# Key projections on an unnormalized residual: a norm deferred past two units of a three-layer kernel

## The chip, the cores and the metric

One core of a Trainium2 chip runs the whole program in one launch. The metric is the device time of that launch in microseconds, as the median of the runs shown. Matrix products run on TensorE (PE), element-wise work on VectorE (DVE), ScalarE (ACT) and GpSimd (POOL), and SyncE's queue (SP) loads the weights. The engines run their own instruction streams in order and meet at semaphores.

## The reference, cut to what matters

Three attention layers follow each other, and a feed-forward layer after the first. The change lies between the second attention layer (differential attention, "A") and the third (windowed grouped-query attention, "B"). The residual is `x` (512 tokens, 1024 features) beside a context `ctx` of 256 tokens.

```
x   = x   + gate_x * (ox @ w_o[0])          # second output projection
ctx = ctx + gate_c * (oc @ w_o[0])
hx  = rms_norm(x,   norm_g[1]) * (1 + scale_x) + shift_x
hc  = rms_norm(ctx, norm_g[1]) * (1 + scale_c) + shift_c
q, k, v, g = split(hx @ w_in)               # 1024, 256, 256, 1024 columns
k   = rope(k); q = rope(q)                  # context keys are not rotated
```

`rms_norm` divides every token by the root of its mean square over the 1024 features. That factor is one number per token, so a product with the unnormalized tile `x * norm_g * (1 + scale_x)` can be multiplied by it afterwards, and the product of `shift_x` with the weights is added as one number per output column.

## The kernel before

**Layout and units.** Features lie on the 128 partitions and tokens in the free dimension, so the residual is `hc`, 8 tiles of 128 features by 768 tokens (512 of `x`, 256 of context). Every projection is cut into units of 128 output columns. A unit multiplies 8 weight tiles by 8 activation tiles; every float32 operand is split into a high and a low part, and `products` (L350) issues three matmuls of 512 (or 256) columns per tile: high by high, high by low, low by high.

**Weights.** SP loads a unit's raw weights into one of four slots. ACT makes the high part (`split_high`, L322, its instruction at L340), POOL the low part (`low`, L986). There are two slots for split weights, so `split_high` of unit u+2 waits until PE has finished unit u. PE waits for the low part.

**Around the change.** The output projection of layer A is done for seven of eight tiles while the heads still run. The last tile follows in `last_out` (L1289): 16 outputs n of three matmuls, 8 for `x` and 8 for the context, each added to `hc` by DVE (L2346). ACT squares the finished tiles (L1752), POOL sums five of them (L1025, L1028), PE sums over features with matmuls of one column (`column_sums`, L422, at L425), ACT takes the root (L431), DVE the reciprocal (L435), and PE spreads it over the partitions into PSUM bank 7 (`spread`, L437, at L440). All engines meet at the end of this phase. Then `modulated` (L2171) makes the normalized tiles one by one: DVE multiplies (`x_tile`, L2039), ACT adds the shift and rounds to the high part (`shift_tile`, L1555), DVE makes the low part (`low_tile`, L2045). PE takes up units 0 and 1 of layer B in `staggered` (L1129), unit 1 six tiles behind unit 0.

**Layer B's 20 units** are 8 for q, 2 for k, 2 for v and 8 for the gate. DVE rotates q and k in PSUM (L2381 to L2387), ACT rounds the high part (`take_b`, L1767, at L1780 or L1783) and DVE subtracts for the low one (L2392, L2396). The units of k and v also have 256 context columns. The context tiles are normalized in pairs during units 3 to 6. `take_b(u)` waits for unit u, splits the weights of unit u+2, and only then waits for the rotation of unit u, so ACT's queue ties the split of later weights to DVE's rotations. The order in every engine's queue is written out by hand.

## Time and profile before

| | us |
|---|---|
| median of 3 runs | 1624.75 |
| lowest and highest run | 1624.64, 1624.96 |
| the profiled execution's own time | 1624.65 |
| its span, first to last instruction | 1622.8 |
| mean granted TensorE clock | 0.986 |

The page of the profile gives each engine's busy time over the span and its share in 40 equal slices, the granted clock of TensorE in tenths, and the chain of work that ended last. The trace answers in more detail: the chain in order of time, single instructions of an engine with their start and duration, and busy time in chosen stretches. Times count from the start of the span.

### The profile page before, as it was taken

How to read it: one execution, taken by the hardware profiler on the slowest of the kernel's cores; microseconds unless marked ns; L12 is line 12 of the kernel's file. 1: busy time of each engine (PE TensorE's matmuls, PEld its weight loads, DVE VectorE, ACT ScalarE, POOL GpSimd, SP SyncE). 2: the span in 40 equal slices, each digit the busy share in tenths (PEclk: the TensorE clock that was granted, in tenths of full speed). 3: DMA queues.
4: the chain of work that ended last, by engine and by line, in shares of the span. 5: the costliest groups of instructions: out<-in, count | busy, mean ns of one | idle time of the engine just before them, and what ended most of it. 6: DMA issues, size and time to landing. Idle time of an engine off the chain costs nothing.

```text
span 1622.8 us, 23738 instructions
## 1 busy us (share of the span) xinstructions
PE 1553.3 (96%) x8400; PEld 1219.6 (75%) x8400; DVE 999.5 (62%) x2286; ACT 757.4 (47%) x1426; POOL 505.3 (31%) x231
## 2 busy tenths in 40 slices
PE   7998999999899999999989999999999989999997
PEld 5886666678688888888877877778777768866666
DVE  6235546355679867645787666675667267147854
ACT  6225676634342323233434544455445443248753
POOL 3651232245244444444221111221114343330012
PEclk9999999999999999999999999999999989999999
DMA  6861111263356665643210111111111122220001
GB/s 201 176 161 34 59 59 63 89 258 130 104 189 196 187 201 188 198 137 94 76 53 27 40 40 39 39 41 36 44 34 53 53 67 86 71 66 15 1 19 60
DMA packets 48402, 149.35 MB, mean 92 GB/s; under 512 B 5782, under 2 KB 9110, under 8 KB 48184
## 3 DMA queue, kind: packets, MB, share of 16 engines
q1 hardware_dynamic: 37080, 112.45, 22.8%
q10 hardware_dynamic: 11232, 35.72, 6.7%
q8 instruction: 54, 0.88, 0.2%
q14 instruction: 36, 0.29, 0.1%
HBM read 141.53 MB, written 6.62 MB: 91 GB/s over the span
## 4 chain that ended last, share of the span: by engine, by line
PE 79%; DVE 8%; ACT 6%; issue 5%; POOL 1%; DMA 1%; ACTq 0%; POOLq 0%; DVEq 0%; SPq 0%
PE ps L357 40%; PE ps L361 19%; PE ps L583 4%; PE ps L594 3%; PE ps L564 3%; PE ps L1336 3%; PE ps L1377 3%; PE ps L1348 1%; POOL w_l L986 1%; ACT sb L649 1%; PE ps L1091 1%; ACT w_h L340 1%; PE ps L425 1%; DVE tg L1972 1%; DVE b_sb L688 1%
## 5 line engine op out<-in xcount | busy, mean ns | idle before, releaser
L986 POOL TENSOR_TENSOR w_l<-raw,w_h 128x1024 fp32r<-128x1024 f32 (+1 forms) x190 | 457.7, 2410 | 894.8 <-ACT w_h L340 874.6
L340 ACT ACTIVATE w_h<-raw 128x1024 fp32r<-128x1024 f32 x190 | 200.5, 1057 | 351.8 <-PE ps L357 293.6
L357 PE MATMUL ps<-x1h,w_h 128*128 128x512 f32 x584 | 237.1, 406 | 16.1 <-POOL w_l L986 10.4
L357 PE MATMUL ps<-x2h,w_h 128*128 128x512 f32 (+2 forms) x784 | 234.0, 361 | 12.3 <-DVE x2l L2045 4.4
L357 PE MATMUL ps<-x1h,w_l 128*128 128x512 f32 x584 | 229.9, 394 | 0.0
L361 PE MATMUL ps<-x1l,w_h 128*128 128x512 f32 x584 | 229.2, 393 | 0.0
L361 PE MATMUL ps<-x2l,w_h 128*128 128x512 f32 (+2 forms) x784 | 221.5, 346 | 0.0
L357 PE MATMUL ps<-x2h,w_l 128*128 128x512 f32 (+2 forms) x784 | 221.2, 345 | 0.0
L357 PEld LDWEIGHTS ps<-x2h,w_h 128*128 128x128 f32 x784 | 126.6, 189 | 41.2 <-issue 12.8
L357 PEld LDWEIGHTS ps<-x2h,w_l 128*128 128x128 f32 x784 | 126.9, 189 | 19.6
L357 PEld LDWEIGHTS ps<-x1h,w_h 128*128 128x128 f32 x584 | 111.0, 190 | 40.4 <-POOL w_l L986 10.8
L361 PEld LDWEIGHTS ps<-x2l,w_h 128*128 128x128 f32 x784 | 126.6, 189 | 18.8
L357 PEld LDWEIGHTS ps<-x1h,w_l 128*128 128x128 f32 x584 | 110.7, 190 | 24.2
L361 PEld LDWEIGHTS ps<-x1l,w_h 128*128 128x128 f32 x584 | 111.2, 190 | 20.4
L2111 DVE CUSTOM_DVE_ANT_0 terms<-mraw,ps 128x1024 f32<-128x1024 f32 x96 | 116.8, 1216 | 2.5
L2280 DVE CUSTOM_DVE_ANT_0 a_p<-ps,small 128x768 f32<-128x768 f32 (+1 forms) x96 | 71.2, 775 | 59.3 <-issue 59.3
L357 PE MATMUL ps<-m_h,w_h 128*128 128x512 f32 x256 | 99.7, 389 | 0.0
L357 PE MATMUL ps<-m_h,w_l 128*128 128x512 f32 x256 | 99.6, 389 | 0.0
L361 PE MATMUL ps<-m_l,w_h 128*128 128x512 f32 x256 | 99.6, 389 | 0.0
L1686 ACT ACTIVATE a_p<-a_p,small 128x768 f32<-128x768 f32 (+1 forms) x96 | 75.2, 785 | 30.9 <-DVE small L2280 30.9
L993 POOL TENSOR_TENSOR g_stage<-g_stage,rstd 128x512 f32<-128x512 f32 x16 | 20.6, 1285 | 147.7 <-ACT g_stage L880 147.7
L688 DVE CUSTOM_DVE_ANT_0 b_sb<-ps,bm 128x512 f32<-128x512 f32 (+1 forms) x64 | 45.9, 753 | 25.9 <-PE ps L564 25.9
(344 smaller groups left out, 2713.5 us busy)
## 6 DMA issues: line engine op xcount, KB each, us to landing
raw<-in_w_mlp SPq DMA_DIRECT2D x64, 512.0 KB, 3.7
mraw<-in_w_mod ACTq DMA_DIRECT2D x51, 512.0 KB, 3.7
raw<-in_w_a SPq DMA_DIRECT2D x32, 512.0 KB, 3.6
raw<-in_w_att SPq DMA_DIRECT2D x25, 512.0 KB, 11.4
raw<-in_w_b SPq DMA_DIRECT2D x20, 512.0 KB, 3.6
raw<-in_w_g SPq DMA_DIRECT2D x16, 512.0 KB, 3.6
raw<-in_w_ao SPq DMA_DIRECT2D x9, 512.0 KB, 3.6
gates<-g_stage ACTq DMA_DIRECT2D x16, 256.0 KB, 2.1
```

The costliest lines, as they stand in the source:

```text
L340: nc.scalar.activation(split(u)[0], raw[:, u % RAW], ACT.Copy).then_inc(w_hi, 1)
L357: mm = nc.tensor.matmul(o, w[:, k], xh(k), start=(first and k == k0 and wi == 0), stop=(last and k == k1 - 1 and wi == 1))
L361: mm = nc.tensor.matmul(o, w[:, k], xl(k), start=False, stop=False)
L564: mm = nc.tensor.matmul(A.sbank(m + h)[:, o:o + rhs.shape[-1]], st[qx](r + h), rhs, start=(x == 0), stop=(x == last), skip_group_check=True)
L583: mm = nc.tensor.transpose(ps[0:w, 4 + x % A.tb, y * P:(y + 1) * P], A.sb[n % A.sbn][:, r, o:o + w], ident[:])
L594: mm = nc.tensor.matmul(ps[h * HD:(h + 1) * HD, 6 + g % 2, cols], st["v"](h)[b], A.pt[0:w, x % 4, h * 2 * P:(h + 1) * 2 * P], start=(st["f ...
L688: nc.vector.tensor_tensor_reduce(out=A.sb[n % A.sbn][:, r, 0:st["keys"]], in0=A.sbank(m)[:, st["off"]:st["off"] + st["keys"]], in1=st["bia ...
L986: nc.gpsimd.tensor_tensor(l[:, ks], raw[:, u % RAW, ks], h[:, ks].bitcast(F32), ALU.subtract).then_inc(w_lo, 1)
L1336: mm = nc.tensor.matmul(pair(1 + 2 * m)[:, o:o + n], aq[ms, qt * P:(qt + 1) * P], ak[ms, key:key + n], start=(x == 0), stop=(x == 2))
L1686: nc.scalar.activation(buf, buf, ACT.Exp, bias=negm[:, cc:cc + 1], scale=-1.0, accum_out=sums[:, cc:cc + 1]).then_inc(ha["e"], 1)
L2111: nc.vector.tensor_tensor_reduce(out=terms[:], in0=mraw[:, c % MRAW].rearrange("p k m -> p (k m)"), in1=cps[:, w, :], scale=0.5, scalar=0. ...
L2280: nc.vector.tensor_tensor_reduce(out=a_p[qt % 3][m][:, 0:n], in0=pair(1 + 2 * m)[:, 0:n], in1=zero.to_broadcast([P, n]), scale=1.0, scalar ...
```

## The change

The two key units move to the front of layer B and read unnormalized tiles of `x` (`xqh`, `xql`) and of the context (new halves in `x2h`, `x2l`). Two columns with the shifts ride along with the context (256 + 2 columns). Their results stay in PSUM banks 0 to 3 and are multiplied by the token factor there, given the shift, and rotated (`rotate_k`). The factor is spread a second time, into bank 4 (bank 6 for the context), and copied to `rstd` by ACT. The first tiles of the first key unit are put among the last outputs of `last_out`. The barriers "heads" and "ao" go. The q units read normalized tiles as before, from the third unit on.

The diff, cut to what sets order and work:

```diff
-        PHASES = ["prep", "wout", "heads", "ao"]
+        PHASES = ["prep", "wout"]
@@ gpsimd
-            add_squares(nm4, SQ_ADDED, 0, S)
             low(U_B)
+            add_squares(nm4, 1, SQ_ADDED, 0, S, sq4[0:2])
             low(U_B + 1)
-            add_squares(nm4c, N_OUT, S, SC)
-            lows(U_B + 2, U_END)
+            add_squares(nm4c, 1, 4, S, SC, sq4c)
+            low(U_B + 2)
+            add_squares(nm4c, 4, N_OUT, S, SC, sq4c)
+            lows(U_B + 3, U_END)
@@ tensor
+            def unscaled_x(j, k0, k1):
+                return products(U_B + j, [(ps[:, 2 * j], lambda k: xqh[:, k, :], lambda k: xql[:, k, :])], k0, k1,
+                                first=(k0 == 0), last=(k1 == KT), ready=lambda k: nm4p.wait(pe, "lo", k + 1))
+            def unscaled_ctx(j):
+                return products(U_B + j, [(ps[:, 2 * j + 1, 0:C + 2], lambda k: x2h[:, k, S:SC + 2], lambda k: x2l[:, k, S:SC + 2])],
+                                ready=lambda k: nm4cp.wait(pe, "lo", k + 1)).then_inc(unit, 1)
+            last_out(0, 12)
+            split_ready(pe, U_B)
+            unscaled_x(0, 0, 1)
+            last_out(12, 14)
+            unscaled_x(0, 1, 2)
+            last_out(14, 16)
+            unscaled_x(0, 2, 6)
+            nm4.wait(pe, "add", SQ_ADDED - 1)
+            column_sums(sqsum, 6, S, True, False)
...
+            mm.then_inc(nm4.mm, 1)
+            unscaled_x(0, 6, KT)
+            split_ready(pe, U_B + 1)
+            unscaled_x(1, 0, 3)
+            nm4.wait(pe, "rc", 1)
+            spread(7, 0, 4).then_inc(nm4.r, 1)
+            spread(4, 0, 4).then_inc(nm4.r, 1)
+            unscaled_x(1, 3, KT)
+            unscaled_ctx(0)
+            unscaled_ctx(1)
-            staggered(pe, U_B, lambda k: nm4.wait(pe, "lo", k + 1), b_parts)
+            for u, between in ((2, ctx_sums), (3, ctx_spreads)):
+                split_ready(pe, U_B + u)
+                if u == 2:
+                    pe.wait_ge(n4_r, 1)
+                products(U_B + u, b_parts(u), 0, 5, last=False, ready=tile)
+                between()
+                products(U_B + u, b_parts(u), 5, KT, first=False, ready=tile).then_inc(unit, 1)
+            for u in range(4, N_B - 2):
...
+                elif u == 4:
+                    pe.wait_ge(n4_r, 2)
+                else:
+                    pe.wait_ge(hb["rot"], (1, 1, 2, 2, 3, 7, 10)[u - 5])
@@ scalar
             for m in range(N_OUT):
                 act.wait_ge(wo_free[1], 2 + m + 1)
+                nc.scalar.activation(xqh[:, m, :], hc[:, m, 0:S], ACT.Copy, scale=mulx[:, 1, 0, m:m + 1]).then_inc(nm4p.hi, 1)
...
             unit_done(act, U_AO_LAST)
-            split_high(act, U_AO_LAST + 2)
-            root(act, nm4, 6, S)
+            split_high(act, U_B + 1)
             for m in range(N_OUT):
+                nc.scalar.activation(x2h[:, m, S:SC], hc[:, m, S:SC], ACT.Copy, scale=mulx[:, 1, 1, m:m + 1]).then_inc(nm4cp.hi, 1)
+                if m == 3:
+                    root(act, nm4, 6, S)
+            nm4.wait(act, "r", 2)
+            nc.scalar.activation(rstd[:, 0:S], ps[:, 4], ACT.Copy).then_inc(n4_r, 1)
+            for m in range(N_OUT):
                 nm4.wait(act, "t", m + 1)
-                shift_tile(m, 1, xn2, 0).then_inc(nm4.hi, 1)
+                shift_tile(m, 1, xn4, 0).then_inc(nm4.hi, 1)
...
+                if m == 4:
+                    unit_done(act, U_B)
+                    split_high(act, U_B + 2)
+            unit_done(act, U_B + 1)
+            split_high(act, U_B + 3)
...
+            root(act, nm4c, 6, C)
+            nm4c.wait(act, "r", 2)
+            nc.scalar.activation(rstd[:, S:SC], ps[:, 6, 0:C], ACT.Copy).then_inc(n4_r, 1)
+            unit_done(act, U_B + 2)
+            split_high(act, U_B + 4)
@@ vector
+            for n in range(2 * N_OUT):
+                finish(n)
+                if n in (11, 13):
+                    unscaled_low((n - 11) // 2)
+            for k in range(2, KT):
+                unscaled_low(k)
...
+            for k in range(KT):
+                nm4cp.wait(v, "hi", k + 1)
+                nc.vector.scalar_tensor_tensor(out=x2l[:, k, S:SC], in0=hc[:, k, S:SC], scalar=mulx[:, 1, 1, k:k + 1],
+                                               in1=x2h[:, k, S:SC].bitcast(F32), op0=ALU.mult, op1=ALU.subtract).then_inc(nm4cp.lo, 1)
+                if k == 3:
+                    invert(v, nm4, S)
+            modulated(nm4, 1, xn4, (0,))
+            rotate_k(0)
+            invert(v, nm4c, C)
+            rotate_k(1)
+            v.wait_ge(n4_r, 2)
+            for u in range(2):
+                y = ps[:, 2 * u + 1, 0:C]
+                done(nc.vector.tensor_tensor(y, y, rstd[:, S:SC], ALU.mult))
+                settle(v)
+                nc.vector.tensor_scalar(y, y, shifted[:, 2 * u + 1:2 * u + 2], None, ALU.add).then_inc(hb["rope"], 1)
+            for u in range(2):
+                v.wait_ge(hb["ev"], u + 1)
+                nc.vector.tensor_tensor(b_kl[:, u, :], pair(u)[:, 0:SC], b_kh[:, u, :].bitcast(F32),
+                                        ALU.subtract).then_inc(hb["rot"], 1)
```

`unscaled_low(k)` is a DVE multiply-subtract from `hc` and `xqh` to `xql`, both inputs in SBUF. `rotate_k(u)` waits for the unit's context part and for `rstd`, copies two shift columns, multiplies the bank by `rstd`, and then does the four operations of a rotation, the shift added in the first two. The weights of the key units are loaded first. After the third new split, `take_b(u)` splits for unit u+2 from u = 3 on.

## Rows read from the trace of the kernel before

**Rows 1.** The page: the chain that ended last, share of the span by engine.
```profile
PE 79%; DVE 8%; ACT 6%; issue 5%; POOL 1%; DMA 1%; ACTq 0%; POOLq 0%; DVEq 0%; SPq 0%
```
**Rows 2.** The chain in order of time, 1288 to 1345: start, length, what.
```profile
1303.25 5.45 PE ps L425 x32
...
1309.25 2.09 PE ps L440 x8
...
1311.43 0.76 DVE xn L2039
...
1323.51 0.50 PE ps L357
```
**Rows 3.** Busy time by stretch; PEclk is the granted clock (last columns: DMA).
```profile
1304.00:1305.00 1.00, 1.00 (x11) 1.00 (x10) 0.00 (x0) 0.49 (x1) 1.00 (x1) 1.00 0.00 0
1305.00:1311.00 6.00, 5.43 (x26) 5.35 (x25) 0.18 (x1) 0.27 (x1) 2.81 (x2) 0.50 0.54 164
1311.00:1318.00 7.00, 4.29 (x10) 2.49 (x10) 6.25 (x9) 4.15 (x9) 1.94 (x3) 0.50 0.02 9
1318.00:1319.00 1.00, 0.89 (x3) 0.17 (x3) 0.96 (x2) 0.89 (x2) 0.29 (x2) 0.68 0.00 0
...
1324.00:1398.60 74.60, 74.60 (x376) 62.75 (x374) 43.52 (x80) 22.14 (x31) 27.46 (x12) 1.00 0.27 85
...
1612.00:1613.00 1.00, 0.58 (x2) 0.58 (x3) 0.18 (x1) 0.16 (x1) 0.00 (x0) 0.60 0.00 0
```
**Rows 4.** ACT's timeline: weight splits behind units of x and of both parts.
```profile
1348.40 1.06 ACT L340 ACTIVATE w_h<-raw 128x1024 fp32r<-128x1024 f32 x1 [1.44 <-PE ps L357]
...
1353.96 1.06 ACT L340 ACTIVATE w_h<-raw 128x1024 fp32r<-128x1024 f32 x1 [2.10 <-PE ps L357]
...
1373.47 1.06 ACT L340 ACTIVATE w_h<-raw 128x1024 fp32r<-128x1024 f32 x1 [5.01 <-PE ps L357]
...
1381.87 1.06 ACT L340 ACTIVATE w_h<-raw 128x1024 fp32r<-128x1024 f32 x1 [4.84 <-PE ps L357]
...
1398.65 1.06 ACT L340 ACTIVATE w_h<-raw 128x1024 fp32r<-128x1024 f32 x1 [6.64 <-PE ps L357]
```
**Rows 5.** DVE's timeline: additions, last tile, a rotation, a key's low part.
```profile
1294.09 8.68 DVE L2346 SCALAR_TENSOR_TENSOR hc<-ps,small,hc 128x512 f32<-128x512 f32 x16 [1.15 <-PE ps L1302]
...
1322.70 1.62 DVE L2045 SCALAR_TENSOR_TENSOR x2l<-xn,small,x2h 128x512 fp32r<-128x512 f32 x2
...
1325.97 0.69 DVE L2381 SCALAR_TENSOR_TENSOR ropeb<-ps,ropeb 128x512 f32<-128x512 f32 x1 [0.97 <-PE ps L357]
...
1328.10 0.70 DVE L2387 TENSOR_TENSOR ps<-ps,ropeb 128x512 f32<-128x512 f32 x1
...
1377.07 0.96 DVE L2396 TENSOR_TENSOR b_kl<-ps,b_kh 128x768 fp32r<-128x768 f32 x1 [0.88 <-ACT b_kh L1783]
```
**Rows 6.** The first layer's deferred norm: ACT's and DVE's halves of an unnormalized tile.
```profile
L1605 ACT ACTIVATE xph<-hc,small x8: 722/724/728, 795.0 to 808.8; 128x512 fp32r<-128x512 f32 x8
L2157 DVE SCALAR_TENSOR_TENSOR xpl<-hc,small,xph x8: 743/746/751, 795.8 to 809.6; 128x512 fp32r<-128x512 f32 x8
```
**Rows 7.** PE's timeline there: four sums, the product behind them, eight spreads, the next product.
```profile
788.76 1.05 PE L425 MATMUL ps<-ones,sq 128*128 128x1 f32 x8
789.68 0.36 PE L357 MATMUL ps<-x2h,w_h 128*128 128x258 f32 x1
...
814.64 1.95 PE L440 MATMUL ps<-ident,small 128*128 128x128 f32 x16
816.35 0.48 PE L357 MATMUL ps<-xph,w_h 128*128 128x512 f32 x1
```
**Rows 8.** POOL's timeline.
```profile
818.25 2.40 POOL L986 TENSOR_TENSOR w_l<-raw,w_h 128x1024 fp32r<-128x1024 f32 x1 [23.81 <-ACT w_h L340]
```
**Rows 9.** DVE's timeline over the same stretch.
```profile
818.00 0.69 DVE L2194 TENSOR_TENSOR ps<-ps,rstd 128x512 f32<-128x512 f32 x1
818.82 2.39 DVE L2045 SCALAR_TENSOR_TENSOR x2l<-xn,small,x2h 128x512 fp32r<-128x512 f32 x1
```

More of the change, by code:

```diff
@@ L1287, in partial_out, with last_out @@
                         mm.then_inc(unit, 1)
-            def last_out():
-                split_ready(pe, U_AO_LAST)
-                pe.wait_ge(ha["lo"], KT)
-                for n in range(2 * N_OUT):
+            def last_out(n0, n1):
+                for n in range(n0, n1):
                     m = n % N_OUT
@@ L1306, in last_out @@
                         mm.then_inc(unit, 1)
-                nm4.wait(pe, "add", SQ_ADDED - 1)
-                column_sums(sqsum, 6, S, True, False)
-                for m in range(SQ_ADDED, N_OUT):
-                    nm4.wait(pe, "sq", m + 1)
-                    mm = column_sums(sq4[m], 6, S, False, m == N_OUT - 1)
-                mm.then_inc(nm4.mm, 1)
-                nm4.wait(pe, "rc", 1)
-                spread(7, 0, 4).then_inc(nm4.r, 1)
             def attend(head, more):
@@ new lines, in _ @@
+            split_ready(pe, U_AO_LAST)
+            pe.wait_ge(ha["lo"], KT)
+            last_out(0, 12)
+            split_ready(pe, U_B)
+            pe.wait_ge(ao_ev0, N_OUT)
+            unscaled_x(0, 0, 1)
[5 more added lines that the diff above has]
+            column_sums(sqsum, 6, S, True, False)
+            for m in range(SQ_ADDED, N_OUT):
+                nm4.wait(pe, "sq", m + 1)
+                mm = column_sums(sq4[m], 6, S, False, m == N_OUT - 1)
@@ L1407, in b_parts, with ctx_sums @@
                     parts.append((ps[:, 2 * (u % 2) + 1, 0:C], lambda k: x2h[:, k, S:SC], lambda k: x2l[:, k, S:SC]))
                 return parts
[L1410 to L1417 removed]
+            def ctx_sums():
+                nm4c.wait(pe, "add", N_OUT - 1)
+                column_sums(sqsum[:, S:SC], 6, C, True, True).then_inc(nm4c.mm, 1)
@@ new lines, in ctx_spreads @@
+            def ctx_spreads():
+                nm4c.wait(pe, "rc", 1)
+                spread(5, 0, 2).then_inc(nm4c.r, 1)
+                spread(6, 0, 2).then_inc(nm4c.r, 1)
+            for u, between in ((2, ctx_sums), (3, ctx_spreads)):
+                split_ready(pe, U_B + u)
+                if u == 2:
+                    pe.wait_ge(n4_r, 1)
+                tile = lambda k: nm4.wait(pe, "lo", k + 1)
+                products(U_B + u, b_parts(u), 0, 5, last=False, ready=tile)
+                between()
+                products(U_B + u, b_parts(u), 5, KT, first=False, ready=tile).then_inc(unit, 1)
@@ L2335, in _, with finish @@
             low(KT - 1)
-            end_phase(v, "heads")
             v.drain().then_inc(wo_free[1], 2)
-            for n in range(2 * N_OUT):
+            def finish(n):
                 m = n % N_OUT
```

125 lines of the change are left out of this document (69 added, 56 removed).

## The prediction

> **What bounds the kernel now.** I read the page first: the chain that ended last lies on PE for 79% of the span [rows 1]. So the question is where PE is late around the change. The chain in order of time shows it [rows 2]: after the last output the sums start at 1303.25 and take 5.45 us, the spreads start at 1309.25 and take 2.09, and then DVE's and ACT's tiles set the pace until the seventh tile's products start at 1323.51. From 1324.0 to 1398.6 PE is busy for all of 74.6 us [rows 3], and DVE for 43.5. So whatever the change gains or loses must show in the time at which the units of layer B that end at 1398.65 [rows 4] are done. Everything behind them is the same work with the same releases and moves with them.
>
> The prices of PE's work come from the pace of ACT's splits, one behind each unit [rows 4]: 5.56 us for a unit of `x` (1348.40 to 1353.96), so 0.695 per tile of three products; 8.40 for a unit with context (1373.47 to 1381.87), so 2.84 for a context part.
>
> From the first output at 1293.1 (0.70 and a hop before DVE's first addition at 1294.09, [rows 5]) to 1398.65 are 105.5 us. Work in it: outputs 8 x 0.695 + 8 x 0.355 = 8.4, and units 8 x 5.56 + 4 x 8.40 = 78.1. So 19 us of the stretch are not products. That is all that there is to win.
>
> **What the change removes.** Two barriers whose cost is hops, and the wait of PE from 1301.9 to 1324.2, in which only seven tiles' products (4.9 us) were done. The half clock from 1305 until 1318.6 [rows 3] fell in that stretch.
>
> **What it adds and moves, in order of time, on the same axis.** I lay out each engine's queue, with 0.1 us for a hop between engines (the end of the spreads at 1311.34 to DVE's start at 1311.43, [rows 2]).
>
> 1. *Outputs and first tiles.* Outputs 0 to 11 end on PE at 1293.1 + 8 x 0.695 + 4 x 0.355 = 1300.1. PE then wants the first unnormalized tile. ACT's half (0.72, [rows 6]) is long done; DVE's stands behind addition 11. The additions take 8.68 for 16 [rows 5], 0.68 and 0.40 apiece, so number 11 ends at 1301.2 and the tile's low part (0.75, [rows 6], plus 0.25 behind a POOL addition) at 1302.1. PE idles 2.0 us, does the tile (0.8) and outputs 12 and 13 (0.7) until 1303.7. DVE, which waited for them, adds (0.9), makes tile 1 (0.75 + 0.15): 1305.3. PE: tile 1, outputs 14 and 15: 1306.9. DVE adds until 1307.7 and makes tile 2: 1308.4. The two interleavings cost two round trips with 1.5 us of idle PE each.
>
> 2. *Tiles 2 to 5.* DVE makes one in 0.67, PE takes 0.695. But ACT splits the weights of unit 1 once output 15 is there (1307.1 to 1308.2), and POOL works on their low part from 1309.0 to 1311.4. Both inputs of DVE's low part lie in SBUF. What that does is to be seen in the first layer: POOL starts at 818.25 and works 2.40 [rows 8]; DVE's instruction, 0.75 elsewhere, starts at 818.82 and takes 2.39, so it ends 0.56 behind POOL's, while DVE's multiplication in PSUM before it takes 0.69 [rows 9]. So tile 5 is held until 1311.95, 1.6 us, and PE ends it at 1312.8.
>
> 3. *Sums.* Sixteen, in a row. Four take 0.92 (788.76 to 789.68, [rows 7]), so 3.7: 1316.5. Root and reciprocal take 0.6, hidden by the next item.
>
> 4. *More tiles, then the spreads.* Tiles 6 and 7 and three of unit 1 are queued ahead of the spreads: 5 x 0.695 = 3.5, 2.8 of it beyond what root and reciprocal need. The first four spreads take 0.86 (half of 1.71 for eight, [rows 7]): the factor is in PSUM at 1320.8. Before it was there at 1309.25 + 2.09 = 1311.34 [rows 2].
>
> 5. *PE on its own.* Four more spreads, five tiles, two context parts: 0.86 + 3.5 + 5.7, until 1330.8. Only the end of the first context part, 1328.0, frees the split slot for unit 2. ACT gets to that split behind its fifth normalized tile, 1328.9; POOL is done at 1332.7. PE idles 2.0. Units 2 and 3, with two sums and four spreads between (0.4 and 0.9) and a wait of 0.5 for the context squares, end at 1345.8. ACT splits for unit 4 only behind the context spreads and their copy, 1344.0, so the weights come at 1347.6: idle 1.9.
>
> 6. *DVE, the chain that I think decides.* From 1320.8 the eight normalized tiles take what they took before, 1311.43 to 1324.3 [rows 2, 5], 12.8, plus 0.75, because ACT first copies the factor, plus 1.5, because POOL's low part for unit 2 holds one of DVE's: 1335.9. The shuffle of the sine table 0.8. Two key rotations: 2.83 for the four old operations (1325.97 to 1328.80, [rows 5]) and 0.8 for a multiplication in PSUM (0.69, [rows 9]) and a copy, 3.65 each. Reciprocal 0.2: 1344.2. Context parts 1.7, two low parts at 0.96 [rows 5] and a wait: 1348.0. Only then the rotation of unit 2: 1350.8. `take_b(2)` waits for it, and `take_b(3)` behind it splits for unit 5: ACT 0.6 + 1.06 [rows 4], POOL 2.40, three hops: 1355.0. PE is done with unit 4 at 1353.6 and idles 1.4. After that DVE needs some 5 us a unit against PE's 5.56 and catches up.
>
> Then PE has five units of `x` and two with context: 5 x 5.56 + 2 x 8.40 = 44.6: the end is at 1399.6 where before it was at 1398.65. **Sum without the clock: +1.0 us.** It is 9.5 later with the factor and only 8.5 shorter behind it.
>
> *The clock.* Before, it fell to half at 1305, while PE did sums, and was back at 1318.6, after 4.7 us of products [rows 3]. Near the end of the kernel sums and spreads likewise brought it down, at 1612 [rows 3]. Here the sums are again sixteen in a row, now with products on both sides. Bounds: it stays, 0; or it falls as early and stays as long as before: then the sums take 6.8 instead of 3.7 (half of them at 0.43, as 5.45 less 1.9 for eight shows [rows 2]: up to +1.6 to +3.1), and the five tiles behind them up to 3.5 more. I take the row nearest to it, a fall, but only for the end of the sums and half of the five tiles, since products resume at once: +1.7. It counts in full, since it delays the factor.
>
> *A page's rule.* The Trainium skill (page "SBUF — State Buffer", section "Who interferes with whom", and its rule of the exclusive lock above it) says that a DVE instruction with two SBUF inputs and a GpSimd instruction exclude each other for a whole instruction. The trace agrees: 2.39 against 0.75 [rows 6, 8, 9]. By it the sum is as above; if DVE were only slowed by half an instruction each time, the two holds would be 2.3 us less and the sum +0.4 with the clock's part. These sentences can be left out.
>
> **The sum against the profiled execution:** 1624.65 + 1.0 + 1.7 = 1627.3. The median of the runs is 0.1 above that execution, so the same number stands for it.
>
> **Rivals.**
> - *The clock stays up* (the rest as above): 1625.7. For it: products on both sides of the sums. Against: both places with a run of sums fell.
> - *PE decides, not DVE* (the other side, faster). If the splits came in time, the idle stretches before units 2, 4 and 5 (2.0, 1.9, 1.4) would go and with them 5.3 us: 1624.65 + 1.0 - 5.3 = 1620.3. It decides if unit 2's rotation ends before 1346.7 and ACT's queue doesn't hold splits 2 and 4. The queue as written speaks against it; DVE's 43.5 busy of 74.6 us [rows 3] for it.
> - *The half clock as before* (clearly slower). PE idles some 5 of 7.5 us at 1300 to 1308. If that brings the clock down before the sums, sums +3.1 and tiles +3.5 come onto the +1.0: 1632.2. It decides if the clock is at half before the sums begin.
> - *DVE and POOL hardly meet*: their order at 1309 and 1330 depends on tenths of a microsecond. Two holds less, 3.1: 1624.2 with the clock's part.
>
> **How the numbers follow.** No change that a measurement of this kernel can tell is within 0.2%, 1621.5 to 1628.0. Chances: forecast 0.40 (its own range 1626.3 to 1629.0, a third of it over 1628.0), clock stays 0.25, PE decides 0.16, half clock as before 0.12, hardly meeting 0.07. Faster 0.16; slower 0.12 + 0.14 + 0.02 from the tail of the second, 0.28; the rest 0.56. The range leaves out the lower half of the faster case and the upper part of the half clock: 1621.0 to 1630.5.
>
> **What would show it.** Right: PE idle about 2 us before the first unnormalized tile and 1.5 twice after; a DVE instruction of about 2.4 in `xql` and one in `x2l`; the factor's spread ending near 1321; idle PE before units 2, 4 and 5 with POOL's low part as releaser; the last unit with context ending 1 to 3 us later than 1398.65. Wrong: DVE idle between 1336 and 1350, or PE without idle time from 1309 to 1360. The prediction falls if DVE's queue is not what unit 5's weights wait for, or if the clock behaves otherwise.

## The result and the profile after

The change is slower by about half a per cent. Median 1633.54 us over 5 runs (1628.64 to 1634.44) against 1624.77 for the kernel before beside it; the ratio is 1.0046 with an interval of 1.0034 to 1.0057. The forecast was 1627.3, and its range ended at 1630.5. In some batches of the experiments a run or two lay far above all others and is left out of the ratios.

The profiled execution happens to be the fastest of the five, 1628.64 us (span 1626.9). Its first output starts at 1293.10, as before (1293.09), so the two timelines can be laid side by side. The other four took 1633.29 to 1634.44. A profile of one such longer execution comes with the first experiment.

The chain that ended last, by engine, as in [rows 1]:

```profile
PE 78%; DVE 8%; ACT 6%; issue 6%; POOL 2%; DMA 1%; POOLq 0%; ACTq 0%; DVEq 0%; SPq 0%
```

The shares hardly moved, so the page alone doesn't show the loss; the timeline does. PE's instructions of the profile after, those that begin after idle time or do the sums and spreads (start, duration, line, then the idle time in brackets and what ended it):

```profile
1302.02 0.47 PE L360 MATMUL ps<-xqh,w_h 128*128 128x512 f32 x1 [1.70 <-DVE xql L2419]
...
1305.05 0.50 PE L360 MATMUL ps<-xqh,w_h 128*128 128x512 f32 x1 [1.39 <-DVE xql L2419]
...
1308.00 0.50 PE L360 MATMUL ps<-xqh,w_h 128*128 128x512 f32 x1 [1.28 <-DVE xql L2419]
...
1311.44 0.67 PE L360 MATMUL ps<-xqh,w_h 128*128 128x512 f32 x1 [1.79 <-DVE xql L2419]
...
1314.05 1.41 PE L428 MATMUL ps<-ones,sqsum 128*128 128x1 f32 x8
...
1317.11 1.03 PE L428 MATMUL ps<-ones,rstd 128*128 128x1 f32 x8
...
1323.12 1.95 PE L443 MATMUL ps<-ident,small 128*128 128x128 f32 x16
...
1335.83 0.50 PE L360 MATMUL ps<-x2h,w_h 128*128 128x512 f32 x1 [1.60 <-POOL w_l L1001]
...
1340.45 0.60 PE L428 MATMUL ps<-ones,sqsum 128*128 128x1 f32 x4 [0.88 <-POOL sqsum L1043]
...
1351.52 0.50 PE L360 MATMUL ps<-x2h,w_h 128*128 128x512 f32 x1 [1.78 <-POOL w_l L1001]
```

In [rows 2] PE begins the sums at 1303.25 and the spreads 0.55 behind their end. Now it has four waits for DVE before the sums, 6.2 us in all, and behind them two for POOL's weights and one for the context squares. The sums begin 1314.05 - 1303.25 = 10.8 us later than before. The fourth wait, before tile 4, is made where DVE and POOL meet. Both engines, same profile:

```profile
1307.20 6.18 DVE L2419 SCALAR_TENSOR_TENSOR xql<-hc,small,xqh 128x512 fp32r<-128x512 f32 x6
...
1324.21 1.41 DVE L2105 SCALAR_TENSOR_TENSOR xn<-hc,small,ps 128x512 f32<-128x512 f32 x2 [3.66 <-PE ps L443]
...
1334.26 2.08 DVE L2111 SCALAR_TENSOR_TENSOR x2l<-xn,small,x2h 128x512 fp32r<-128x512 f32 x1
...
1353.78 0.70 DVE L2502 TENSOR_TENSOR ps<-ps,ropeb 128x512 f32<-128x512 f32 x1
```

```profile
1307.97 2.86 POOL L1001 TENSOR_TENSOR w_l<-raw,w_h 128x1024 fp32r<-128x1024 f32 x1 [3.53 <-ACT w_h L343]
...
1333.22 2.55 POOL L1001 TENSOR_TENSOR w_l<-raw,w_h 128x1024 fp32r<-128x1024 f32 x1 [1.66 <-ACT w_h L343]
...
1356.13 2.40 POOL L1001 TENSOR_TENSOR w_l<-raw,w_h 128x1024 fp32r<-128x1024 f32 x1 [4.66 <-ACT w_h L343]
```

Six low parts take 6.18 where six at 0.75 would be some 4.1 (they overlap a little; a version without the meeting shows 4.05 below): one of them waits out POOL's 2.86. The second meeting shows in the row of 2.08 for a tile of `x2l`. ACT's splits behind the rotation of unit 2 and behind unit 11:

```profile
1355.00 1.05 ACT L343 ACTIVATE w_h<-raw 128x1024 fp32r<-128x1024 f32 x1
```
```profile
1403.62 1.06 ACT L343 ACTIVATE w_h<-raw 128x1024 fp32r<-128x1024 f32 x1 [6.64 <-PE ps L360]
```

The last unit with context is done at 1403.6, where it was 1398.65 [rows 4]: 5.0 us later. The spans differ by 4.1: 0.9 came back near the end, where the last spreads take 3.56 before, all at half clock, and 2.50 after.

The granted clock, in windows of 4 us (length, busy time of PE, weight load, DVE, ACT and POOL, then the clock, DMA share, GB/s), first the profile after:

```profile
1311.00:1315.00 4.00, 3.56 (x12) 2.98 (x12) 3.93 (x10) 0.00 (x0) 0.00 (x0) 0.58 0.47 131
1315.00:1319.00 4.00, 4.00 (x31) 3.83 (x32) 0.69 (x3) 0.82 (x3) 0.00 (x0) 0.93 0.00 0
1319.00:1323.00 4.00, 4.00 (x13) 3.15 (x12) 1.55 (x4) 1.03 (x3) 0.00 (x0) 0.64 0.00 0
```

The number before the last two is the granted clock as a share of 2.4 GHz; 0.5 is the lower level of 1.2 GHz. A window's length times one less the clock is the time lost: 1.7 + 0.3 + 1.4 = 3.4 us before the factor. That way of reading splits the time to the first normalized tile into a part of the queues and one of the clock. It holds as long as the path runs through PE's work while the clock is at half; where PE would have waited for DVE anyway, half clock costs nothing. I use it for every run below, in windows of half a microsecond.

### The profile page after: what moved, and what is told of

Read it like the earlier page. It is cut to its first block, busy times and chain, and to the rows that moved or that the text cites. A ratio compares the mean times of both kernels' runs of the same rounds, so it can differ in the third digit from the quotient of the medians.

```text
span 1626.9 us, 23787 instructions
## 1 busy us (share of the span) xinstructions
PE 1553.9 (96%) x8412; PEld 1221.2 (75%) x8412; DVE 1015.4 (62%) x2312; ACT 765.6 (47%) x1444; POOL 506.9 (31%) x231
## 4 chain that ended last, share of the span: by engine, by line
PE 78%; DVE 8%; ACT 6%; issue 6%; POOL 2%; DMA 1%; POOLq 0%; ACTq 0%; DVEq 0%; SPq 0%
PE ps L360 39%; PE ps L364 19%; PE ps L591 4%; PE ps L602 3%; PE ps L572 3%; PE ps L1342 3%; PE ps L1383 3%; POOL w_l L1001 1%; PE ps L1354 1%; ACT sb L657 1%; PE ps L1108 1%; ACT w_h L343 1%; DVE tg L2038 1%; PE ps L428 1%; DVE b_sb L696 1%
## 5 line engine op out<-in xcount | busy, mean ns | idle before, releaser
L360 PE MATMUL ps<-x1h,w_h 128*128 128x512 f32 x584 | 237.4, 406 | 15.3 <-POOL w_l L1001 10.4
L360 PE MATMUL ps<-x2h,w_h 128*128 128x512 f32 (+2 forms) x768 | 229.6, 360 | 11.1 <-POOL w_l L1001 3.4
L364 PE MATMUL ps<-x2l,w_h 128*128 128x512 f32 (+2 forms) x768 | 217.8, 345 | 0.0
L360 PE MATMUL ps<-x2h,w_l 128*128 128x512 f32 (+2 forms) x768 | 217.5, 344 | 0.0
L360 PEld LDWEIGHTS ps<-x1h,w_h 128*128 128x128 f32 x584 | 111.4, 191 | 38.9 <-POOL w_l L1001 10.8
```

Source lines behind the costliest of these rows:

```text
L360: mm = nc.tensor.matmul(o, w[:, k], xh(k), start=(first and k == k0 and wi == 0), stop=(last and k == k1 - 1 and wi == 1))
L364: mm = nc.tensor.matmul(o, w[:, k], xl(k), start=False, stop=False)
```

## The experiments

For each run three things were read beside its time: **T**, from the first output to DVE's first normalized tile (31.1 in the profile after, 18.3 before); **L**, the half-clock loss in T; and **U**, from the first output to the split behind unit 11 (110.5 after, 105.6 before). T less L is the queues' part. Runs of one batch shared a chip and its runs of the kernel before.

| run | T | L | T - L | U | median us | ratio to before, interval |
|---|---|---|---|---|---|---|
| kernel before | 18.3 | 3.2 | 15.1 | 105.6 | | |
| after, as first profiled | 31.1 | 3.4 | 27.7 | 110.5 | 1633.5 | 1.0046 (1.0034 to 1.0057) |
| the change again | 34.3 | 6.8 | 27.5 | 113.7 | 1633.4 | 1.0041 (1.0028 to 1.0055) |
| all waits filled | 31.2 | 3.4 | 27.8 | 110.5 | 1629.5 | 1.0017 (1.0008 to 1.0026) |
| outputs first | 27.3 | 3.4 | 23.9 | 106.6 | 1626.7 | 1.0001 (0.9992 to 1.0010) |
| split of unit 4 early | 31.0 | 3.4 | 27.6 | 111.9 | 1632.8 | 1.0042 (1.0028 to 1.0055) |
| spreads first | 31.8 | 6.4 | 25.4 | 112.9 | 1633.6 | 1.0043 (1.0031 to 1.0055) |
| POOL late | 27.4 | 1.7 | 25.7 | 106.8 | 1626.9 | 1.0006 (0.9998 to 1.0015) |
| splits 4 and 5 early | 34.3 | 6.8 | 27.5 | 114.3 | 1635.1 | 1.0056 (1.0043 to 1.0069) |
| four orders together | 23.2 | 1.7 | 21.5 | 104.5 | 1626.5 | 1.0001 (0.9992 to 1.0009) |
| fourth wait filled | 31.2 | 3.4 | 27.7 | 110.5 | 1630.6 | 1.0027 (1.0017 to 1.0038) |
| POOL late, DVE held by two | 30.6 | 3.4 | 27.1 | 109.9 | 1630.0 | 1.0023 (1.0012 to 1.0034) |
| splits through | 24.0 | 2.8 | 21.2 | 102.7 | 1622.4 | 0.9981 (0.9972 to 0.9990) |
| splits through, filled | 24.4 | 3.0 | 21.4 | 102.9 | 1621.9 | 0.9977 (0.9968 to 0.9986) |
| POOL late, DVE held by three | 34.5 | 6.8 | 27.7 | 113.9 | 1631.0 | 1.0031 (1.0019 to 1.0043) |
| tiles between the sums | 25.1 | 3.0 | 22.1 | 102.9 | 1623.7 | 0.9988 (0.9979 to 0.9997) |

Before's medians in the four batches were 1626.4, 1625.3, 1626.3 and 1625.1. T, L and U are of one profiled execution each, which need not be the median one.

**The change again.** No edit.

> The changed kernel once more, for a second profile, since its runs spread from 1628.6 to 1634.4 us while the kernel before has 1624.6 to 1626.4. Theory A (TensorE's clock): the short idle stretches around the deferred norm let the clock fall in more places in some executions; the profile then shows more half-clock stretches than the three of the first one (1311.8, 1318.4, 1352.8), and the time follows their number. Theory B (queues alone): two profiles agree within 1 us, and the spread comes from elsewhere.

The median held. This profile's first output comes at 1294.69, 1.6 us later than in the profile after. Half clock ahead of it took 1.6 us more (15.3 against 13.7), in falls that lie outside the change. The same windows as above, in this profile:

```profile
1311.00:1315.00 4.00, 2.21 (x6) 1.61 (x6) 4.00 (x5) 0.05 (x1) 1.39 (x1) 0.78 0.25 95
1315.00:1319.00 4.00, 4.00 (x19) 3.81 (x19) 1.86 (x6) 0.00 (x0) 0.00 (x0) 0.50 0.09 36
1319.00:1323.00 4.00, 4.00 (x18) 3.90 (x19) 0.18 (x1) 0.61 (x3) 0.00 (x0) 0.50 0.00 0
1323.00:1327.00 4.00, 4.00 (x11) 3.09 (x11) 1.68 (x4) 1.25 (x4) 0.00 (x0) 0.51 0.00 0
```

Half clock from 1313 to 1327: 0.9 + 2.0 + 2.0 + 2.0 = 6.8 lost, and the first normalized tile 3.2 later than in the profile after, at the same T - L. From there to the split behind unit 11 both take 79.4 us to the hundredth. So the delay of the factor comes out at the end undiminished. Both profiles lose another 1.7 us to half clock some 60 us behind the first output, behind the factor; U - T is no shorter, 79.3, in profiles without that fall (all waits filled, outputs first, below), so it costs nothing there.

**All waits filled.** 34 unread products of 512 columns, spread over the six waits of PE:

```diff
+            nm4p.wait(pe, "hi", 1)
+            filler(7, 7)
             unscaled_x(0, 0, 1)
             last_out(12, 14)
+            filler(7, 5)
             unscaled_x(0, 1, 2)
...
```

> The changed kernel with 34 extra products of 512 columns whose result nothing reads, put into the six places where PE waits (before unnormalized tiles 0, 1, 2 and 4, and before the weights of units 2 and 4), as many as the wait seen there holds. Theory A (clock): the clock stays up at least at 1311 and 1352, so the time falls by 2 to 6 us below the changed kernel in spite of the added work, and the runs spread less. Theory B (queues decide when DVE is done, PE's speed in between is hidden): no gain, within 1 us, or a loss of up to 2.

3.9 us of the median came back (1633.4 to 1629.5) with nothing earlier in the queues (T - L 27.8). In the profile the clock stayed up at tile 4 and fell in the second half of the sums. The runs didn't draw together, as theory A had it: eleven lie between 1626.1 and 1631.5. And L is 3.4, no less than in the profile after, so the gain must lie in the executions that lose more; that was not profiled.

**Outputs first.**

```diff
-            last_out(0, 12)
+            last_out(0, 16)
             split_ready(pe, U_B)
             pe.wait_ge(ao_ev0, N_OUT)
-            unscaled_x(0, 0, 1)
-            last_out(12, 14)
-            unscaled_x(0, 1, 2)
-            last_out(14, 16)
-            unscaled_x(0, 2, 6)
+            unscaled_x(0, 0, 6)
```

> The changed kernel with the 16 last outputs and their 16 additions in one piece, and the first unnormalized tiles only behind them. In the laid-out queues the two round trips between PE and DVE go: additions end near 1302.8 instead of 1307.3, tile 5 is done some 5 us earlier, and the factor too. Theory B (DVE's chain behind the factor decides): about 4 to 5 us faster than the changed kernel. Theory A (clock first): a gain of the same size or more, since one wait of about 2 us takes the place of four. Rival C (the interleaving pays because it fills PE): 1 to 3 us slower than the changed kernel.

T is 3.8 us less than in the profile after, at the same L, and the kernel is level with before. The two round trips are gone, but the meeting of DVE and POOL is not. The path in this profile:

```profile
1303.51 7.14 DVE xql L2415 x6
...
1310.70 0.50 PE ps L360
...
1311.66 3.46 PE ps L428 x32
```

Six low parts take 7.14 in the place of 4.05, and tile 5 waits for the last of them. The clock was at half from 1306 to 1309.5, so PE was late for that tile anyway and waits only 0.17. Here half clock and hold lie over each other, and T - L is 1.7 too small: the queues' part is 25.6, and the two round trips cost 27.7 - 25.6 = 2.1.

**Split of unit 4 early**, ahead of the copy of the context's factor.

```diff
             root(act, nm4c, 6, C)
-            nm4c.wait(act, "r", 2)
-            nc.scalar.activation(rstd[:, S:SC], ps[:, 6, 0:C], ACT.Copy).then_inc(n4_r, 1)
             unit_done(act, U_B + 2)
             split_high(act, U_B + 4)
+            nm4c.wait(act, "r", 2)
+            nc.scalar.activation(rstd[:, S:SC], ps[:, 6, 0:C], ACT.Copy).then_inc(n4_r, 1)
```

> The changed kernel with ACT's split of unit 4's weights ahead of its wait for the context factor. PE's 1.8 us before unit 4 go. Theory B (DVE's chain decides, unit 5's weights come when unit 2 is rotated): 0 to 1 us, since unit 5 then waits instead. Theory A (clock): the fall at 1352.8, which followed that wait, goes too: 2 to 4 us faster.

No gain: U - T is 80.9. PE's wait before unit 4 is gone, and so is the fall of the clock that followed it, but this wait stands before unit 5 in its place:

```profile
1360.17 0.50 PE L360 MATMUL ps<-x2h,w_h 128*128 128x512 f32 x1 [3.19 <-POOL w_l L1001]
```

Behind it the clock is at half from 1361 to 1364.5, 1.7 us lost, and U - T is 1.5 longer.

**Spreads first.**

```diff
-            unscaled_x(1, 0, 3)
             nm4.wait(pe, "rc", 1)
             spread(7, 0, 4).then_inc(nm4.r, 1)
             spread(4, 0, 4).then_inc(nm4.r, 1)
-            unscaled_x(1, 3, KT)
...
+            unscaled_x(1, 0, KT)
```

> The kernel after the change, with the two sets of spreads put directly behind tiles 6 and 7 of unit 0, ahead of the three tiles of unit 1 (same work, other order in PE's queue). The three tiles are 3 x 0.695 = 2.1 us. Theory B (the queues: the factor's arrival starts DVE's chain, and that chain ends at the split behind unit 11 some 79.4 us later, as in four of the five profiles of the change so far): the first normalized tile on DVE comes 29.0 us behind the first output instead of 31.1, the split behind unit 11 at some 108.5 instead of 110.5, and the kernel is 2 us shorter than after (some 1631.4 where after measured 1633.4). Root and reciprocal then show as a small idle stretch of PE, up to 0.7. Theory A (the half clock alone makes the loss, the queue order doesn't matter): no gain, 1633 again, or a loss if the idle stretch makes the clock fall. Rival C (weights of later units set the time, not DVE): x_tile earlier by 2 but the split behind unit 11 where it was.

The factor came 2.1 earlier in the queues, as worked out, but U - T grew by 1.7 to 81.1: rival C in part. The three tiles stand behind the spreads now, so units 0 and 1 end as late as ever, and ACT meets them in the middle of the normalized tiles:

```profile
1335.44 1.06 ACT L343 ACTIVATE w_h<-raw 128x1024 fp32r<-128x1024 f32 x1 [1.36 <-PE ps L360]
```

This is the split of unit 2, which waits for unit 0. In the profile after it came without a wait (1332.10). Here ACT stands 1.36 before it, with the sixth tile queued behind, and DVE takes 27.4 us from its first normalized tile to the keys' low parts instead of 25.7.

**POOL late.** The low part of unit 1 only behind DVE's eighth unnormalized tile.

```diff
             add_squares(nm4, 1, SQ_ADDED, 0, S, sq4[0:2])
+            nm4p.wait(g, "lo", KT)
             low(U_B + 1)
```

> The kernel after the change, with POOL's low part of unit 1's weights begun only when DVE has done the eighth unnormalized tile, so that the two don't meet. Theory of the lock: the DVE instruction in xql that took 2.4 us goes back to 0.75, PE's wait of 1.8 before tile 4 goes, and the sums come 1.6 earlier; by theory B the first normalized tile and the kernel's end come 1.6 earlier too (1631.8 where after measured 1633.4). Rival: POOL's low part, then 2.4 us later, is late for unit 1's first tile and PE waits there instead, before the spreads: half of it or all is lost again (0 to -0.8). If POOL's hold was only a slower DVE and not a lock, the same gain; but if other instructions of DVE now take 2.4, the hold has only moved.

The ratio went from 1.0041 to 1.0006, some 6 us, over three times the delay of 1.8. DVE's six tiles in this profile:

```profile
1309.16 4.05 DVE L2420 SCALAR_TENSOR_TENSOR xql<-hc,small,xqh 128x512 fp32r<-128x512 f32 x6
...
1313.33 2.34 DVE L2431 TENSOR_TENSOR x2l<-small,x2h 128x16 fp32r<-128x16 f32 x1
```

4.05 in the place of 6.18, so 1.8 of queue (T - L 25.7 against 27.5 in the profile of the change again). T itself is 6.9 less: the other 5.1 are the clock, L being 1.7 where it was 6.8. The meeting itself has only moved, to an instruction of 16 columns (2.34) that nobody on the path waits for. PE's wait before tile 4 went with it, and the clock fell only at 1317, behind the sums.

**Splits of units 4 and 5 early.** In addition to the edit of the split of unit 4:

```diff
             def take_b(u):
 
-                if u >= 3:
-                    unit_done(act, U_B + u)
-                    split_high(act, U_B + u + 2)
+                if u == 2 or u > 3:
+                    v = 3 if u == 2 else u
+                    unit_done(act, U_B + v)
+                    split_high(act, U_B + v + 2)
```

> The kernel after the change, with the splits of units 4 and 5 both taken out from behind what they wait for on ACT: that of unit 4 ahead of the copy of the context factor, that of unit 5 ahead of the wait for unit 2's rotation. By the prediction, unit 5's weights wait for DVE's chain through this split, so PE's wait before unit 4 (1.8) and before unit 5 (1.4 forecast) both go. If the weights are the tie between DVE's chain and PE: 1.5 to 3 us shorter than after (1630.4 to 1631.9 where after measured 1633.4), with x_tile where it was and the split behind unit 11 earlier than 79.4 us behind it, about 77. If DVE's chain ties PE directly (unit 5 and 6 wait for the PSUM banks that the rotations free), nothing is gained: 1633, with PE waiting for the rotation at unit 5 or 6 instead of for POOL. Splitting unit 4 alone gave 1632.8 with a distance of 80.9.

Nothing gained. The waits before units 4 and 5 are gone, and one stands before unit 6, whose split is behind the rotation of unit 3. So the tie is DVE's chain through ACT's queue, at the first split that still stands behind a rotation:

```profile
1366.44 0.79 PE L360 MATMUL ps<-x2h,w_h 128*128 128x512 f32 x1 [2.50 <-POOL w_l L1001]
```

**Four orders together:** outputs first, spreads first, POOL late, splits of 4 and 5 early.

> Four orders changed together in the kernel after the change: outputs first and the unnormalized tiles behind them, both sets of spreads behind tiles 6 and 7, POOL's low part of unit 1 behind DVE's eighth unnormalized tile, and the splits of units 4 and 5 early. Theory B adds the savings: from the version with outputs first alone (1626.7, factor use at 27.3 behind the first output) another 2.1 for the spreads, 0 to 1.6 for the lock (with the outputs first DVE may be past its tiles already), 0 to 2 for the splits: 1621 to 1624.5, below the kernel before (1626.4). Theory A (the clock decides and takes its 3 to 6 us wherever it falls): 1626 to 1629, no better than before, with half clock in the records between the sums and unit 2.

T - L is 6.2 less than in the change, but the median is only level with before. U is 104.5: the same wait of 2.5 before unit 6, and with its end at 1357.5 the clock falls, to half until 1361. The profiled run, 1623.4, is one of the shorter ones of 1623.0 to 1627.8.

**Fourth wait filled.** The filler of the second run in the wait before tile 4 alone.

```diff
-            unscaled_x(0, 2, 6)
+            unscaled_x(0, 2, 4)
+            nm4p.wait(pe, "hi", 5)
+            filler(7, 6)
+            unscaled_x(0, 4, 6)
```

> The kernel after the change, with six unread products of 512 columns (6 x 0.23 = 1.4 us) put into PE's fourth wait alone, the one of 1.8 us before tile 4 that DVE's 2.4-us instruction makes. DVE and POOL still meet there and the tile comes no earlier; only PE is busy meanwhile. Theory A' (that fourth idle stretch is what brings the clock down before the sums, as in the profile where it was at half from 1312 to 1327 and the first normalized tile came 34.3 behind the first output): the clock is up through tiles 4 and 5 and most of the sums, x_tile at 31 or a little under, and the kernel is some 3 to 4.5 us shorter than the change as it is (1629 to 1630.5 where that measured 1633.4), as with all six waits filled (1629.5). Theory L (POOL's hold costs by its delay alone and through nothing else): no gain, 1633. Rival: the earlier idle stretches of 1.7, 1.4 and 1.3 bring the fall: no gain either, half clock from 1312 on.

The clock fell in the last quarter of the sums and not before tile 4; PE's idle time there is 0.45, and T - L is unchanged. The granted clock again in windows of 4 us (this profile's first output is at 1294.33):

```profile
1312.00:1316.00 4.00, 3.55 (x25) 3.00 (x24) 3.93 (x9) 0.00 (x0) 0.09 (x1) 1.00 0.41 131
1316.00:1320.00 4.00, 4.00 (x21) 3.71 (x21) 1.61 (x5) 1.50 (x5) 0.00 (x0) 0.62 0.00 0
```

The median is 2.8 below that of the change again, against equal medians of before (1626.3 and 1626.4), more than half of what filling all six gave. But the interval of the ratio, 1.0017 to 1.0038, overlaps both that of the change (1.0028 to 1.0055) and that of all six filled, so the time by itself doesn't settle it.

**POOL late, DVE held by two.** In addition to the edit of "POOL late":

```diff
                 nm4p.wait(v, "hi", k + 1)
+                if k == 4:
+                    for _ in range(2):
+                        done(nc.vector.scalar_tensor_tensor(out=ropeb[:, 0, :], in0=hc[:, k, 0:S], scalar=mulx[:, 1, 0, k:k + 1],
+                                                            in1=xqh[:, k, :].bitcast(F32), op0=ALU.mult, op1=ALU.subtract))
+                        settle(v)
```

> The version with POOL's low part of unit 1 begun late, which took back 6.5 us, with the delay put back by other means: DVE does two unread instructions of 0.75 ahead of the fifth unnormalized tile, so PE waits there some 1.8 again, without DVE and POOL meeting. Theory A' (idle PE brings the clock down, whoever makes it idle): all is lost again, 1632 to 1634, half clock from 1312 to 1327. Theory L (the meeting itself does more harm than its delay, for instance to DVE's other instructions): only the delay of 1.5 is lost, 1628.5. By the delay and half of the clock's part: in between, which would say that the fall comes in some executions and not in others.

In between. The idle stretch came out at 1.25, not 1.8, and the clock fell at the end of the sums. About half of what "POOL late" had taken back was lost again (1630.0 against 1626.9, on another chip).

**Splits through.** The four orders, with the splits of units 5 to 9 early.

```diff
-                if u == 2 or u > 3:
-                    v = 3 if u == 2 else u
+                if 2 <= u < 7 or u > 7:
+                    v = u + 1 if u < 7 else u
```

> The version with four orders changed, with ACT's splits taken out from behind DVE's rotations for units 5 to 9, not 5 alone. In that version PE's largest wait was 2.5 us for POOL's low part of unit 6, whose split stood behind the rotation of unit 3 (1353.44) while unit 4 had been done at 1349.7. If the tie between DVE's chain and PE is ACT's queue: this wait goes and none takes its place at units 7 to 9, the split behind unit 11 comes 102 us behind the first output instead of 104.5, and the kernel is 2.5 to 3 shorter than that version (1623.5 to 1624 where that measured 1626.5), about at the kernel before (1625.3) or just below it. Rival (the PSUM banks that the rotations free hold PE at unit 5 or 7): a wait for DVE in the place of the one for POOL and no gain, 1626.5. Rival (the clock takes it back: the fall that came with the 2.5 us of idle time comes elsewhere): 1626.

Faster than both kernels: 1622.4 against 1626.3, ratio 0.9981 (0.9972 to 0.9990). U is 102.7, and nothing like the last wait took its place: behind these, one of 0.62 at 1380.57 is left, before unit 10, whose split stands behind a rotation again. PE's idle stretches from 1316 to 1365 in this profile, all of them:

```profile
1332.61 0.50 PE L360 MATMUL ps<-x2h,w_h 128*128 128x512 f32 x1 [0.82 <-POOL w_l L1001]
1337.23 0.61 PE L428 MATMUL ps<-ones,sqsum 128*128 128x1 f32 x4 [0.89 <-POOL sqsum L1043]
```

**Splits through, filled.** Six and two unread products before tiles 0 and 1.

```diff
+            nm4p.wait(pe, "hi", 1)
+            filler(7, 6)
             unscaled_x(0, 0, 1)
+            filler(7, 2)
             unscaled_x(0, 1, 6)
```

> The same as the version with the splits of units 5 to 9 early, and six and two unread products of 512 columns in PE's waits before the first two unnormalized tiles (1.4 and 0.5 us of 1.7 and 0.7), to keep PE from being idle ahead of the sums. If idle PE brings the clock down, the half clock between 1306 and 1310 goes (0.5 x 3 us, more in the executions where it lasts): 1 to 3 us under the version without them, 1621 to 1623.5, faster than the kernel before. If that fall is not owed to these two waits: no gain, or 0.3 lost for products that start late.

The fall some 12 us behind the first output is gone, but one that begins 18.4 behind it, at the sums, is as long as both were (3.4 us lost in all in both profiles). The gain of 0.5 us is within the intervals.

**POOL late, DVE held by three.** The hold with `range(3)`.

> The version with POOL's low part of unit 1 begun late and DVE held ahead of the fifth unnormalized tile, now with three unread instructions of 0.75 in the place of two. With two, PE's fourth wait was 1.25 us, the clock fell only at the end of the sums, and the first normalized tile came 30.55 behind the first output. With three the wait is 1.9, a little more than the 1.79 that the meeting of DVE and POOL made. Theory A' (the length of PE's idle stretch there decides whether the clock falls at tile 4 or at the end of the sums): the fall moves to tile 4, the half clock takes some 6.8 instead of 3.4 us before the first normalized tile, which comes at 34.5 to 34.9, and the kernel is 4 us longer than with two: 1633.5 to 1634.5. Theory L (only the meeting of the two engines brings the early fall): the added delay of 0.65 and no more, x_tile at 31.2, 1630.5.

The profile came out as theory A' had it: PE's wait is 2.03, T 34.5, L 6.8, the same as the change with the meeting, but with no meeting:

```profile
1308.27 1.41 DVE L2425 SCALAR_TENSOR_TENSOR xql<-hc,small,xqh 128x512 fp32r<-128x512 f32 x2
1309.59 2.32 DVE L2422 SCALAR_TENSOR_TENSOR ropeb<-hc,small,xqh 128x512 f32<-128x512 f32 x3
1311.95 2.74 DVE L2425 SCALAR_TENSOR_TENSOR xql<-hc,small,xqh 128x512 fp32r<-128x512 f32 x4
```
```profile
1312.75 0.50 PE L360 MATMUL ps<-xqh,w_h 128*128 128x512 f32 x1 [2.03 <-DVE xql L2425]
```

The granted clock, of the version held by two and then of this one:

```profile
1313.00:1317.00 4.00, 3.44 (x25) 3.15 (x25) 3.97 (x6) 0.00 (x0) 1.43 (x1) 1.00 0.00 0
```
```profile
1312.00:1316.00 4.00, 3.25 (x11) 2.72 (x12) 3.97 (x6) 0.00 (x0) 1.23 (x1) 0.65 0.00 0
1316.00:1320.00 4.00, 4.00 (x20) 4.00 (x20) 2.81 (x5) 0.00 (x0) 1.11 (x1) 0.50 0.41 112
```

The median did not: 1631.0, with twelve runs from 1625.8 to 1634.7, and the ratio's interval overlaps that of the version held by two. The profiled run, 1633.1, is one of the longer ones. So the early fall doesn't need the meeting, but with this order it seems not to come in every execution.

**Tiles between the sums.** From "splits through": tile 6 behind the first four sums, tile 7 behind the next four, one tile of unit 1 ahead of the spreads.

```diff
+            unscaled_x(0, 6, 7)
             for m in range(SQ_ADDED, N_OUT):
                 nm4.wait(pe, "sq", m + 1)
                 mm = column_sums(sq4[m], 6, S, False, m == N_OUT - 1)
+                if m == SQ_ADDED:
+                    unscaled_x(0, 7, KT)
             mm.then_inc(nm4.mm, 1)
-            unscaled_x(0, 6, KT)
+            split_ready(pe, U_B + 1)
+            pe.wait_ge(wo_free[1], 2 + 2 * N_OUT)
+            unscaled_x(1, 0, 1)
```

> The fastest order so far (splits of units 5 to 9 early, outputs first, spreads early, POOL late; 1622.4), with tiles 6 and 7 of unit 0 put between the sixteen sums instead of behind them and one tile of unit 1 ahead of the spreads. In all five of the last profiles the clock also fell at the end of the sums or at the spreads, and filling PE's waits ahead of them did not change that. Theory S (the sums themselves, columns of one, bring that fall): with products among them it doesn't come; the 1.3 to 3.4 us of half clock before the first normalized tile go, against 0.7 for the tile ahead of the spreads: 1620 to 1621.5. Rival (the fall comes all the same, a little later): 0.7 to 1.4 lost, 1623 to 1624.

The rival: 1623.7, L 3.0. The clock fell between the last sums and the spreads all the same, and T - L is 0.9 longer, some 0.7 of it the tile ahead of the spreads. Theory S falls.

## Why the prediction was wrong

The queues were laid out nearly right. The term for the clock, 1.7, was half of what the profile after lost and a quarter of what the second profile lost.

1. *Outputs and first tiles: right.* Idle before tile 0 is 1.70 (2.0 forecast), then 1.39 and 1.28 (1.5 each); PE takes tile 2 at 1308.00 (1308.4).
2. *Tiles 2 to 5: mechanism right, price wrong.* The hold is 1.8 us of PE (1.6 forecast), one tile earlier, at tile 4 and not at 5. But I counted it only as a delay. Its removal gave some 6.
3. *Sums.* 3.95 long (3.7 forecast), 1.3 late from the half clock in tiles 4 and 5. Their first third is at half clock too; at full clock they take 3.46 (in "outputs first").
4. *The factor.* 27.7 behind the first output forecast (1320.8 - 1293.1) and 0.1 to DVE; T - L is 27.7 and 27.5. Right, in part because the errors above are small and of both signs.
5. *PE on its own.* 2.0, 0.5 and 1.9 idle were forecast before unit 2, the context sums and unit 4; 1.60, 0.88 and 1.78 came. The 1.4 before unit 5 doesn't show in either profile of the change, because half clock made unit 4 longer there. Where the clock was up (both fillings, outputs first, held by two) that wait is 1.22 to 1.25.
6. *DVE's chain: right.* From the factor to the end of unit 2's rotation 30.0 was forecast and is 30.3 (1324.21 to 1354.48); to unit 5's weights 34.2, and 34.3 came; to the last unit with context 78.8 against 79.4. That the chain acts through ACT's queue is shown by the runs that move the splits: the wait went from unit 4 to 5 to 6 and all but disappeared with "splits through".

Sum without the clock: +1.0 forecast. The runs give 27.7 + 79.4 = 107.1 against 105.6, so +1.5.

**The step that failed is the clock's.** I took "a fall, but only for the end of the sums and half of the five tiles": 1.7. It measured 3.4 us in the profile after and 6.8 in that of the change again. With them: 1624.65 + 1.5 + 3.4 - 0.9 for the end of the kernel = 1628.65, which is the profiled run; that is no test, since the 0.9 is what the same two profiles leave over. And 1624.65 + 1.5 + 6.8 = 1633.0, or 1632.1 with that 0.9, against a median of 1633.5. The second profile's own time, 1633.4, has the 1.6 of half clock ahead of the change besides. Only these two executions of the change were profiled, so that the other long ones lost 6.8 in the same place rests on their times. Their mean granted clocks, 0.984 to 0.987, don't follow the times: the run of 1633.12 has 0.987, the profile after 0.986.

The median is nearest to the rival that had 0.12, *the half clock as before*, 1632.2. Its condition, half clock before the sums begin, is met in both profiles of the change; the length that it took, as long as before, is met only in the second. Its reason was in the text (PE idles 5 of 7.5 us; 4.4 of 7.7 came), but the forecast took the sums for the cause, since both places that it read in the trace of before had sums in them. That trace shows the clock in more places, and two of them speak for idle PE. In the first layer's deferred norm eight lots of sums stand among products without a wait, and the clock stays up; at 844 it falls with no sums near, some 2.5 us into a wait of 7.4:

```profile
796.00:814.00 18.00, 18.00 (x114) 15.96 (x113) 14.15 (x22) 9.25 (x16) 0.00 (x0) 1.00 0.08 26
...
842.00:844.00 2.00, 0.00 (x0) 0.00 (x0) 1.97 (x5) 1.46 (x2) 0.46 (x1) 1.00 0.22 90
844.00:846.00 2.00, 0.00 (x0) 0.00 (x0) 2.00 (x1) 0.00 (x0) 1.88 (x1) 0.55 0.00 0
```

What brings the clock down ahead of the sums is idle PE before tile 4. In the six profiles where that wait was 1.8 to 2.0 (the two of the change, unit 4 early, spreads first, units 4 and 5 early, held by three) the clock fell 18.4 to 19.0 us behind the first output, at tile 4. In the four where it was filled, short or absent (both fillings, POOL late, held by two) it fell at 21.9 to 22.4. With the outputs first it fell at 11.5 to 12.2, where PE waits 1.7 for tile 0 and 0.7 for tile 1, and not when those waits were filled. An early fall isn't always dearer: of the six, two lost 3.4 us before the factor and four 6.4 to 6.8; the four later falls lost 3.4 or, with POOL late, 1.7.

What stays open is the fall around the sums and spreads. It came in every version, with PE idle ahead of them or busy, and with products among the sums; no edit here removed it. Open too is what makes one execution lose 3.4 and another 6.8 with the same instructions: the runs show both, and their profiles don't say why. The same shows outside the change: at 791, in the first layer, where two lots of sums and the spreads follow each other with a wait of 0.3 or less, the clock falls in three of the sixteen profiles (the change again, unit 4 early, POOL late) and stays up in the others, at the same work. Nor does the length of one wait decide alone: the change waits the same 1.7 for tile 0 as the versions with the outputs first, and has no fall there.

## What to carry to other kernels

An idle stretch of PE has two prices, its own length and the clock that it may bring down; count the second wherever several waits of 1 to 2 us follow each other, even if each looks harmless: here a wait of 1.8 stood for some 6. A norm deferred behind the product moves the start of the element-wise work later (here the first normalized tile from 18.3 to 31.1 us behind the first output), so the element-wise chain behind the factor has to be loosened too. Of the orders tried, only those with the outputs in one piece, the spreads ahead of all or most of unit 1's tiles, POOL's low part late and the splits of units 4 to 9 early came out below the kernel before, by 0.1 to 0.2%; which of the four are needed was not separated. When a wait moves from unit 4 to 5 to 6 as splits are moved, cut the tie for all of them at once.

## What the runs showed of the hardware

- The same kernel gave 1628.6 and 1633.4 in its two profiled executions, and up to the last unit with context they differ in the half clock alone: 1.6 us more lost ahead of the change, and 3.4 or 6.8 before the factor, at the same queue schedule within 0.2.
- An idle stretch of 1.25 before tile 4 left the clock up there and one of 2.03 did not, at the same work around it, in one profile each.
- A DVE subtraction of two SBUF inputs with only 16 columns, 0.18 us alone in the profile after (1313.50), takes 2.34 when POOL's low part runs beside it (1313.33 in "POOL late", where POOL's instruction starts at 1313.29 and takes 2.35). So 16 columns are held as long as the 512 of a tile (2.39 in [rows 9]).
